# An expert-retrieval layer: tile 0's scatter from group 35, one-hots made ahead, VectorE operands in a PSUM bank

## The reference, cut to what matters

```python
def peer_layer(x, wq, keys, U, Vt):          # 256 tokens, 8 heads, D = 2048
    q = (xt @ wq).reshape(T, 8, 2, 128)
    scores = einsum('thcd,hcnd->thcn', q, keys)
    s_top, i_top = top_k(scores, 16)         # per head and half
    cand = s_top[:, :, 0, :, None] + s_top[:, :, 1, None, :]
    best, pos = top_k(cand, 16)              # 16 of 256
    idx = i_top[..., 0] * 128 + i_top[..., 1]    (at pos)
    gate = softmax(best)
    hid = gelu(einsum('td,thkd->thk', x, U[idx]))
    return einsum('thk,thkd->td', gate * hid, V[idx])
```

## Time and profile before

| what | us |
|---|---|
| median of 3 runs (2172.59 to 2183.35) | 2181.03 |
| the profiled execution, its own time | 2163.77 |
| its span | 2162.1 |
| DVE busy in the span | 1644.0 (76%) |
| PE busy | 1476.4 (68%) |
| POOL busy | 973.0 (45%) |
| ACT busy | 835.0 (39%) |

### The profile page before, as it was taken

The page is one execution under the profiler, slowest core; times in us unless marked ns, Lnnn a source line. Parts: engine busy times, 40 slices in busy tenths (PEclk is TensorE's granted clock), DMA queues, the critical chain, the costliest instruction groups (busy, mean ns, idle before and its releaser), DMA issues.

```text
span 2162.1 us, 26403 instructions
## 1 busy us (share of the span) xinstructions
PE 1476.4 (68%) x9809; PEld 1369.3 (63%) x9809; DVE 1644.0 (76%) x2174; ACT 835.0 (39%) x1006; POOL 973.0 (45%) x691
## 2 busy tenths in 40 slices
PE   6999999999999999800000000113358999999996
PEld 6987998898999889800000000113347999999996
DVE  4465764545644557699988899998878999999997
ACT  4344432344333444212112221346676444444443
POOL 1002220000000000288888878877647676667763
PEclk9999999999999999955555555555579999999998
DMA  5555444434455555799999999999805999999996
GB/s 195 176 175 179 152 137 137 157 129 160 167 176 176 195 176 173 267 410 422 421 420 412 402 389 406 415 403 367 348 14 203 355 357 358 357 371 359 359 357 227
DMA packets 151526, 597.80 MB, mean 276 GB/s; under 512 B 14688, under 2 KB 14704, under 8 KB 118000
## 3 DMA queue, kind: packets, MB, share of 16 engines
q0 software_dynamic: 58048, 356.02, 41.6%
q1 hardware_dynamic: 93360, 240.22, 32.2%
HBM read 594.09 MB, written 2.10 MB: 276 GB/s over the span
## 4 chain that ended last, share of the span: by engine, by line
PE 41%; issue 22%; POOL 15%; DVE 12%; DMA 5%; ACT 4%; POOLq 0%; DVEq 0%; SPq 0%; ACTq 0%; PEldq 0%
POOL starts L506 10%; PE acc L1505 8%; PE acc L1508 8%; PE acc L1507 8%; DVE slots L1314 5%; POOL slots L469 4%; PE acc L1522 3%; PE scr L1775 3%; PE acc L1524 3%; PE acc L1523 3%; DMA slots<-in_peer_u,expert 3%; DMA starts<-in_v_gather,expert 1%; PE scr L1570 1%; ACT weight_of L739 1%; DVE w_lo L817 1%
## 5 line engine op out<-in xcount | busy, mean ns | idle before, releaser
L817 DVE TENSOR_TENSOR w_lo<-raw,w_hi 128x2048 fp32r<-128x2048 f32 x136 | 314.6, 2314 | 311.3 <-ACT w_hi L522 310.1
L1314 DVE SCALAR_TENSOR_TENSOR slots<-slots,acc 128x2048 f32<-128x2048 f32 x188 | 423.9, 2282 | 23.2 <-DMA slots<-in_peer_u,expert 21.3
L522 ACT ACTIVATE w_hi<-raw 128x2048 fp32r<-128x2048 f32 x136 | 260.1, 1913 | 441.2 <-PE acc L1508 297.5
L506 POOL DMA_INDIRECT starts<-in_v_gather,expert x256 | 344.4, 1345 | 153.1 <-DVE X L1446 99.0
L469 POOL DMA_INDIRECT slots<-in_peer_u,expert x256 | 253.8, 992 | 278.0 <-DVE expert L1286 148.4
L1505 PE MATMUL acc<-hT_hi,w_hi 128*128 128x256 f32 x1024 | 294.1, 287 | 3.1 <-PE acc L1508 2.5
L1775 PE MATMUL scr<-hot_a,hot_b 128*128 128x128 f32 x512 | 102.1, 367 | 281.2 <-ACT hot_a L751 172.4
L477 POOL TENSOR_TENSOR slots<-slots,N 128x2048 f32<-128x2048 f32 x62 | 281.8, 4546 | 24.5 <-DMA slots<-in_peer_u,expert 23.5
L1507 PE MATMUL acc<-hT_lo,w_hi 128*128 128x256 f32 x1024 | 291.8, 285 | 0.0
L1508 PE MATMUL acc<-hT_hi,w_lo 128*128 128x256 f32 x1024 | 291.6, 285 | 0.0
L790 ACT ACTIVATE v_hi<-v_raw 128x1408 fp32r<-128x1408 f32 x128 | 177.0, 1383 | 280.0 <-PE scr L1807 208.1
(11 more groups left out here) (262 smaller groups left out, 3326.1 us busy)
## 6 DMA issues: line engine op xcount, KB each, us to landing
raw<-in_w_in SPq DMA_DIRECT2D x88, 1024.0 KB, 5.0
v_raw<-in_v_dense SPq DMA_DIRECT2D x128, 704.0 KB, 6.3
raw<-in_w_o SPq DMA_DIRECT2D x16, 1024.0 KB, 5.0
raw<-in_peer_wq SPq DMA_DIRECT2D x16, 1024.0 KB, 5.2
raw<-in_w_a_up SPq DMA_DIRECT2D x8, 1024.0 KB, 5.0
raw<-in_w_b_up SPq DMA_DIRECT2D x8, 1024.0 KB, 5.0
slots<-in_peer_u,expert POOLq DMA_INDIRECT x256, 8.9
starts<-in_v_gather,expert POOLq DMA_INDIRECT x256, 6.6
```

The lines of the kernel that those rows point to most:

```text
L506: pool.indirect_dma_start(starts[s % CRING][:, :], None, v_gather[:, :], bass.IndirectOffsetOnAxis(ap=expert[:, s // NSEL, s % NSEL:s % NS ...
L522: a.activation(w_hi[:, m % 2, :, :], raw[:, m % 2, :, :], ACT.Copy).then_inc(hi_ready, 1)
L817: v.tensor_tensor(w_lo[:, m % 2, :, :], raw[:, m % 2, :, :], w_hi[:, m % 2, :, :].bitcast(fp32), ALU.subtract).then_inc(lo_ready, 1)
L1314: v.scalar_tensor_tensor(out=slots[j][:, :], in0=slots[j][:, :], scalar=1.0, in1=row, op0=ALU.mult, op1=ALU.mult, accum_out=hid_sum[:, t, ...
```

## The change

It does eight things.

1. `SPREAD_FROM` is 35 and `SPREAD_TWICE` 57: tile 0's batches go one a group from 35 to 56, two a group from 57 to 61, none in 62 and 63.
2. `parts(g)`: the selection takes five parts in four groups (two in each fourth group) and ends at group 41; `IJ_GROUP` is 45.
3. ACT makes tile 0's A one batch ahead: `hot_first(0, 0)` at group 33, then `hot_first(0, n + 1)` before `scatter_out(0, n)`.
4. ACT makes A of tile 1's first eight batches in groups 47 to 54, before the gates exist.
5. `hot_a1` has eight places, four of them in the selection's old room.
6. Of the other 24 batches of tile 1 POOL makes 18, ACT three (11, 19, 27) and DVE three (15, 23, 31), up to eight batches ahead.
7. Half of a `scr` bank (`vbank`) keeps the index rows (`iota`), the top places as floats, the second half's top scores, the decoded places, the second index and the expert number, so that those operations of DVE have one operand or their result in PSUM. Two small copies a pair are added (`top_second`; `ij` from its column).
8. The gates' transposition goes to the other half of `scr`; PE's waits follow.

```diff
 PIECES = 4
-SPREAD_FROM, SPREAD_TWICE = 44, 52
-IJ_GROUP = 56
+SPREAD_FROM, SPREAD_TWICE = 35, 57
+IJ_GROUP = 45
+AHEAD_FROM = 47
+PLACES = 8
...
     first = max(0, min(g, SPREAD_TWICE) - SPREAD_FROM) + twice
-    return range(first, first + (g >= SPREAD_FROM) + (g >= SPREAD_TWICE))
+    return range(min(BATCHES, first), min(BATCHES, first + (g >= SPREAD_FROM) + (g >= SPREAD_TWICE)))
+def parts(g):
+    first = 3 + g + (g + 3) // 4
+    return range(min(56, first), min(56, first + 1 + (g % 4 == 0)))
+def maker(n):
+    return "dve" if n % PLACES == 7 else "act" if n % PLACES == 3 else "pool"
...
         hot_a, hot_b = carve("hot_a", 2, SC, P), carve("hot_b", 2, SC, P)
-        hot_a1 = at("hot_a1", 160, [4, SC, P])
+        hot_a1 = [at(f"hot_a1_{n}", kib, [SC, P]) for n, kib in enumerate((160, 162, 164, 166, 184, 188, 190, 192))]
...
         scr = ctx.enter_context(nc.psum_tensor("scr", [P, 2, 2 * GW], fp32))
+        vbank = scr[:, 1, 0:GW]
+        iota_ps, iota16_ps = vbank[:, 0:P], vbank[:, P:P + TOPK]
+        topf_ps = vbank[:, 144:208].rearrange("p (h c k) -> p h c k", h=2, c=2)
+        top_second = vbank[:, 208:240].rearrange("p (h k) -> p h k", h=2)
+        bpos_ps = vbank[:, 240:304].bitcast(u32).rearrange("p (c m) -> p c m", c=2)
+        ij_ps, expert_ps = vbank[:, 304:336], vbank[:, 336:368]
...
-            for n in range(0, BATCHES, 2):
-                pool.wait_ge(hot_used, BATCHES + n - 1)
-                pool.sem_inc(granted, 1)
-                for c in range(SC):
-                    last = g.tensor_scalar(hot_a1[:, n % 4, c, :], iota_p, ijT[:, 1, 0, n * SC + c:n * SC + c + 1], None,
-                                           ALU.is_equal)
-                last.then_inc(a_ready[1], 1)
+            pool.wait_ge(ij_ready, 2)
+            for n in range(PLACES, BATCHES):
+                if maker(n) == "pool":
+                    pool.wait_ge(hot_used, 2 + BATCHES + n - PLACES + 1)
+                    pool.sem_inc(granted, 1)
+                    for c in range(SC):
+                        last = g.tensor_scalar(hot_a1[n % PLACES][:, c, :], iota_p, ijT[:, 1, 0, n * SC + c:n * SC + c + 1],
+                                               None, ALU.is_equal)
+                    last.then_inc(a_ready[1], 1)
...
-                act.wait_ge(hot_used, BATCHES + n - 1 if t else 1 + n)
-                to = hot_a1[:, n % 4, :, :] if t else hot_a[:, n % 2, :, :]
+                if t == 0:
+                    act.wait_ge(hot_used, 1 + n)
+                elif n >= PLACES:
+                    act.wait_ge(hot_used, 2 + BATCHES + n - PLACES + 1)
+                to = hot_a1[n % PLACES][:, :, :] if t else hot_a[:, n % 2, :, :]
...
                 last.then_inc(a_dist, 1)
-                act.wait_ge(a_dist, BATCHES + n // 4 + 1 if t else n + 1)
+                made[0] += 1
+                act.wait_ge(a_dist, made[0])
...
+            made = [0]
...
                     act.wait_ge(ij_ready, 1)
+                    hot_first(0, 0)
                 for n in spread(i):
-                    hot_first(0, n)
+                    if n + 1 < BATCHES:
+                        hot_first(0, n + 1)
                     scatter_out(0, n)
+                if i == AHEAD_FROM:
+                    act.wait_ge(ij_ready, 2)
+                if AHEAD_FROM <= i < AHEAD_FROM + PLACES:
+                    hot_first(1, i - AHEAD_FROM)
...
-            act.wait_ge(ij_ready, 2)
             for n in range(BATCHES):
-                if n % 4 == 0:
-                    hot_first(1, n + 3)
+                if n + 6 < BATCHES and n + 6 >= PLACES and maker(n + 6) == "act":
+                    hot_first(1, n + 6)
...
                 tv = topv[:, us, :].rearrange("p (h c) k -> p h c k", c=2)
-                tf = topf[:, us, :].rearrange("p (h c) k -> p h c k", c=2)
+                if t or pair:
+                    places, second, tops = iota16_ps, top_second, topf_ps
+                    decoded, column, flat = bpos_ps, ij_ps, expert_ps
+                else:
+                    places, second, tops = iota16[:, :], None, topf[:, us, :].rearrange("p (h c) k -> p h c k", c=2)
+                    decoded, column, flat = bpos[:, 1:3, ks], None, bposf[:, 2, ks]
...
                 if part == 4:
-                    link(v.tensor_copy(topf[:, us, :], topi[:, us, :]))
+                    link(v.tensor_copy(tops, topi[:, us, :].rearrange("p (h c) k -> p h c k", c=2)))
+                    if second is None:
+                        second = tv[:, :, 1, :]
+                    else:
+                        link(v.tensor_copy(second, tv[:, :, 1, :]))
...
                     link(v.tensor_tensor(cands, tv[:, :, 0, :].unsqueeze(3).to_broadcast([P, 2, TOPK, TOPK]),
-                                         tv[:, :, 1, :].unsqueeze(2).to_broadcast([P, 2, TOPK, TOPK]), ALU.add))
+                                         second.unsqueeze(2).to_broadcast([P, 2, TOPK, TOPK]), ALU.add))
...
                 if part == 6:
-                    v.tensor_scalar(bpos[:, 1, ks], bpos[:, 0, ks], 4, None, ALU.logical_shift_right)
-                    link(v.tensor_scalar(bpos[:, 2, ks], bpos[:, 0, ks], TOPK - 1, None, ALU.bitwise_and))
-                    link(v.tensor_copy(bposf[:, 0:2, ks], bpos[:, 1:3, ks]))
+                    v.tensor_scalar(decoded[:, 0, :], bpos[:, 0, ks], 4, None, ALU.logical_shift_right)
+                    link(v.tensor_scalar(decoded[:, 1, :], bpos[:, 0, ks], TOPK - 1, None, ALU.bitwise_and))
+                    link(v.tensor_copy(bposf[:, 0:2, ks], decoded))
...
                     link(v.tensor_tensor(hots, bposf[:, c, ks].unsqueeze(2).to_broadcast([P, 2 * TOPK, TOPK]),
-                                         iota16[:, :].unsqueeze(1).to_broadcast([P, 2 * TOPK, TOPK]), ALU.is_equal))
-                    link(v.tensor_tensor(hot4, hot4, tf[:, :, c, :].unsqueeze(2).to_broadcast([P, 2, TOPK, TOPK]),
+                                         places.unsqueeze(1).to_broadcast([P, 2 * TOPK, TOPK]), ALU.is_equal))
+                    link(v.tensor_tensor(hot4, hot4, tops[:, :, c, :].unsqueeze(2).to_broadcast([P, 2, TOPK, TOPK]),
                                          ALU.mult))
-                    link(v.tensor_reduce(ij[:, t, c, ks], hots, AX.X, ALU.add))
+                    if c == 1 and column is not None:
+                        link(v.tensor_reduce(column, hots, AX.X, ALU.add))
+                        link(v.tensor_copy(ij[:, t, 1, ks], column))
+                    else:
+                        link(v.tensor_reduce(ij[:, t, c, ks], hots, AX.X, ALU.add))
                 if part == 7:
-                    link(v.scalar_tensor_tensor(out=bposf[:, 2, ks], in0=ij[:, t, 0, ks], scalar=float(P),
-                                                in1=ij[:, t, 1, ks], op0=ALU.mult, op1=ALU.add))
-                    v.tensor_copy(expert[:, t, ks], bposf[:, 2, ks]).then_inc(expert_ready, 1)
+                    link(v.scalar_tensor_tensor(out=flat, in0=ij[:, t, 0, ks], scalar=float(P),
+                                                in1=ij[:, t, 1, ks] if column is None else column,
+                                                op0=ALU.mult, op1=ALU.add))
+                    v.tensor_copy(expert[:, t, ks], flat).then_inc(expert_ready, 1)
...
             copy_scores(3)
+            v.tensor_copy(iota_ps, iota_p)
+            link(v.tensor_copy(iota16_ps, iota16[:, :]))
...
                     token = slice(n * SC + c, n * SC + c + 1)
-                    last = v.tensor_scalar(hot_b[:, n % 2, c, :], iota_p, ijT[:, t, 1, token], gateT[:, t, token],
+                    last = v.tensor_scalar(hot_b[:, n % 2, c, :], iota_ps, ijT[:, t, 1, token], gateT[:, t, token],
...
-                dve.wait_ge(hot_used, BATCHES + n - 1)
-                v.tensor_tensor(hot_a1[:, n % 4, :, :], iota_p.unsqueeze(1).to_broadcast([P, SC, P]),
+                dve.wait_ge(hot_used, 2 + BATCHES + n - PLACES + 1)
+                v.tensor_tensor(hot_a1[n % PLACES][:, :, :], iota_ps.unsqueeze(1).to_broadcast([P, SC, P]),
...
                 dve.wait_ge(gate_landed, t + 1)
-                v.tensor_copy(gateT[:, t, :], scr[:, 1, 0:P]).then_inc(gateT_ready, 1)
+                v.tensor_copy(gateT[:, t, :], scr[:, 0, 0:P]).then_inc(gateT_ready, 1)
...
                         dot(q)
-                    if q % FOUR == 1 and i + 3 < IJ_GROUP:
-                        later_part(i + 3)
+                    if q % FOUR == 1:
+                        for n in parts(i):
+                            later_part(n)
...
             for n in range(BATCHES):
-                if n % 4 == 1:
-                    hot_first(n)
+                if n + 6 < BATCHES and n + 6 >= PLACES and maker(n + 6) == "dve":
+                    hot_first(n + 6)
...
                 if t:
-                    pe.wait_ge(ij_ready, t)
+                    pe.wait_ge(gateT_ready, t)
...
             def turn_gate(t):
+                pe.wait_ge(ij_ready, t + 1)
```

(10 more changed lines are left out.)

## The result

The changed kernel takes **2147.08 us** (median of four runs, 2145.23 to 2148.63) where the kernel before takes 2177.63 (four runs, 2172.59 to 2183.35): a ratio of 0.9859, 95% interval 0.9829 to 0.9888, 30.5 us less. The forecast was 2152, 29 less, within 2139 to 2173. So the gain is 20 to 30 us. That the first series gave 30.5 where 29 had been forecast is in part luck: its runs of the kernel before were some 7 us slower than those of the later series. I therefore judge the steps by stages and not by the median alone.

A forecast was written before the change was run, and what follows sets the result against it. The gather stage was taken as bound by memory at 10.0 us a group, with slower stretches and a late end. Gathers -13, end -17 and tile 1's scatter +1 gave -29 us from 2181: 2152, range 2139 to 2173.

The forecast's parts named there:

- The doubled groups: Gather groups with two tile 0 batches each: ScalarE's wait for TensorE goes, and the whole 19.5 us comes back.
- The end: Last gather's issue to tile 1's first one-hot: 17.5 us where it was 34.6, so 17 less (bounds 12 and 20).
- The switch: Change of tiles at group 32 and groups to 41: VectorE gets more work, 6 us more lost (bounds 0 to 12).
- The faster selection: Gather stage up to group 31: VectorE at 9.5 us a group stays under the memory's 10.0, so no cost.
- Gathers together: Whole gather stage: the last gather is issued 13 us earlier (bounds 5 and 20).
- The price of a PSUM operand: VectorE's one-hots reading PSUM: 0.3 us each (bounds 0.28 and 0.41).
- Rival D: VectorE's one-hots read PSUM slowly, 0.56 us each, tile 1 becomes bound by VectorE: +21 us, 2202; chance 0.04.
- Tile 1's scatter: Scatter stage of tile 1: bound by POOL's 18 batches, 49 to 50.5 us against 49.6, +1 us (bounds -1 and +6).
- The stalls: VectorE's selection operation held behind POOL's products: 4.65 us falls to about 0.2 with one operand in PSUM.
- B, the switch eats the gain: VectorE late in groups 32 to 41: last gather's issue gains only 3, total -16 us, 2165; chance 0.18.
- C: POOL slower in tile 1's scatter, 2.71 us a batch, +6.5 there: total -23 us, 2158; chance 0.12.
- E: TensorE's matmuls stay at 1.2 GHz throughout tile 1's scatter: +27 us, 2179, no change; chance 0.03.

The follow-up runs named there:

- old schedule, no A ahead: Changed kernel with the old batch and selection numbers, and tile 0's first one-hots made just before their own batch's copy: 2176.25 us, ratio 1.0021.
- before again: The kernel before the change, rerun with no edit: 2168.94 us, ratio 0.9995.
- the old schedule: Changed kernel with the old numbers (one batch a group from 44, two from 52, slower selection), everything else new: 2140.04 us, ratio 0.9871.
- the second profile: Profile of the changed kernel rerun with no edit on another chip: 2146.93 us, ratio 0.9886.
- Tile 1's B from SBUF: Changed kernel with VectorE's second one-hots of tile 1 reading the index row from SBUF again: 2142.88 us, ratio 0.9862.

## Why the prediction was right

**The doubled groups, 19.5 back: right in size, the cause only one of two.** From group 52 to the last issue the two profiles of the change take 113.7 and 114.7 us, those of before 133.3 and 133.4: 19.2 less in the mean. The reason is the one given. The same groups with the wait of ScalarE put back cost it all again (old schedule, no A ahead). What I had not seen: with only five doubled groups the ring of rows would have hidden four of them. Without A ahead the change still takes 119.7 us there, 13.7 less than before and not 19.2. So in this change the schedule alone does for most of the gain, as A ahead alone does in the old one; the prediction gave all of it to A ahead.

**The end, 17 less: 15.7.** The sum of 17.5 had its parts nearly right: from the last issue to the last dot 11.7 us and not 10.9, and from the gate's subtraction to the first B 4.4 and not 4.3 (1564.88 to 1569.26).

**The switch, 6 more lost: 3 to 5.** The first profile shows 15.0 over pace against 10.3, the second 11.7 against 8.7 of before again. (The prediction's words give group 34 a batch; its sum rightly has none.) But the reference was wrong: with the stalls gone, the old schedule loses only 4 there (123.8, 123.9), not 10.3. The bank gives about 5.5 at the switch, and starting at 35 takes 8 to 11 away again. I had summed both into one number, and saw the balance and not the two effects; that the balance came out near is luck.

**The faster selection costed at nothing: wrong by about 4 us.** This is the step that failed. "With the dots 9.5: under 10.0" is a mean over four groups. In the first eight the rows of the ring have just been filled, and at group 3 POOL waited 4.59 us for VectorE's dots, where it waits 1.0 with one part in group 0. Groups 0 to 7 take 105 us in the mean of the seven kernels with this selection's pace, 101 in the six others, before and before again among them. Of these 4 us, 2.5 lie in groups 2 to 7 (62.9 against 60.4), where the cause is seen; the rest lies in groups 0 and 1, which differ by 3 us between two kernels with the same code, and isn't shown. From 8 to 31 the cost is within 1 us, as I said.

**Gathers together, 13 less: 8.9 and, in the second profile, 6.8.** That is within the bounds of 5 and 20.

**The price of a PSUM operand: 61 ns, not 22.** The one-hot from PSUM takes 401 ns against 340 from SBUF in the median of before, and in tile 1's scatter 401 against 364. The two numbers that I compared were of different kinds: 278 is a quarter of four overlapping one-hots, each of which lasts 340, and 285 is the whole duration of a single copy. The 0.3 that came of it was too low as a duration (0.33 from one one-hot's start to the next); the upper bound of 0.41 held. The Trainium skill, "VectorE: DVE Perf Modes", sections on the TRN2 errata and on PSUM operands, puts the fixed term of a PSUM source at 120 cycles against 58 and allows it no doubled mode for fp32, 0.13 us more by an estimate from that page. The runs show half of that; of the 3.7 us of loss, 1.7 appear in tile 1's scatter. Rival D, at 0.56 an operation, is ruled out.

**Tile 1's scatter, +1: +1.6, for the wrong reason.** The size was right and POOL ran without a gap, but TensorE waited for VectorE. One-hots from PSUM follow each other every 0.33 us (10.67 / 32), so eight batches are 12.15 us of VectorE, not 10.3, and 32 are 48.6 of the 51.2. POOL needs more for eight batches (6 x 2.31 = 13.9), but makes 18 batches in all while VectorE makes B of 32: 41.6, begun 3.8 after the first B and ended 5.8 before the end. I had compared the two by their eight batches, as if POOL had them all to make. Tile 1's B from SBUF moves the scatter by 1.7: the next limit is that near.

**The stalls: right.** 0.196 us for the operation that had taken 4.65. The Trainium skill, "SBUF — State Buffer", section on the two separate sides, says that VectorE with two inputs in SBUF and GpSimd shut each other out of a shared pair of ports for a whole instruction. The rows agree for VectorE: 4.65 us before, as long as POOL's product of 4.5, and none longer than 0.2 with one input in PSUM. That POOL is held in turn, no row here shows.

**The rivals.** B, the switch eats the gain, did not come: 8.9 and 6.8 are more than its 3. C would have POOL at 2.71 a batch; it was 2.31. E, the clock staying at 1.2 GHz, did not come: the granted clock rose from 0.50 to 1.00 3.4 us after the scatter's first matmul, against 4.9 before. The sum of the profiles' touched stages is -8.9 - 15.7 + 1.6 = -23.0, against -29. So the mechanism held and the sum was 6 us too high, 4 of them in the gather stage; the 30.5 of the medians looks nearer only because it contains 7 us or so by which that series' runs of before were slower than those of the later ones.

## What to carry to other kernels

Where one engine makes an operand, waits for the engine that uses it, and copies the result before it makes the next, make the next operand first: here that one line of order gave as much alone (30 us) as it and the new table of numbers together, and the table alone gave 22. Two remedies for the same loss don't add up, so a change that holds both has to be taken apart in all four combinations before either is called the cause. Before giving an engine more work in a stretch that runs at the memory's pace, look at its sum group by group from the points where buffers are empty or full (the start, a switch), since a mean below the pace hides waits there. Before operands are moved to escape a stall, look in which stretch the stalled operations lie: the one-hots' stalls here lay where the engine had slack. And before a limit is named by who runs without a gap, read who the last engine waits for: two engines can both be full.

## What was unexpected

- An operand in PSUM costs VectorE 61 ns on 128 elements (340 to 401), but makes the duration steady: 396 to 410 where SBUF gave 331 to 2585. In the mean over the kernel both forms are equal (407 and 402) or PSUM is ahead (510 without it in the changed kernel).
- POOL's own one-hots got faster when VectorE read from PSUM: 594 ns in the change, 612 with tile 1's B from SBUF.
- The kernel before differs by up to 10 us between series (medians 2167.17 to 2177.63), while the change had 2147.08 and 2146.93. I have no cause for that; a gain in one series is known to about 10 us.
